# Two edits of order in a two-block transformer kernel: the opening (small loads behind the first roundings, more identity turns), and the place of the last maxima of each attention head on VectorE

## The reference

```python
def rmsnorm(x, g):
    xf = x.astype(jnp.float32)
    y = xf * lax.rsqrt(jnp.mean(xf * xf, axis=-1, keepdims=True) + EPS)
    return (y * g.astype(jnp.float32)).astype(x.dtype)

def even_mixer(h, layer, w_in, ...):
    p = jnp.einsum('bsd,de->bse', h, w_in)
    da_q, da_k, da_v, da_z, ml_qk, ml_v, ml_i, ml_f, ml_o, ml_z = _split(p, EVEN_SIZES)
    lam = (exp(dot(lambda_q1, lambda_k1)) - exp(dot(lambda_q2, lambda_k2)) + lam_init)
    ...
        s = jnp.einsum('bhcqd,bhckd->bhcqk', qi, kt)          # qi scaled, 8 heads, c = 2
        s = jnp.where(k_pos[None, :] <= q_pos[:, None], s, -jnp.inf)
        p = jax.nn.softmax(s, axis=-1)
        a = p[:, :, 0] - lam * p[:, :, 1]
        return jnp.einsum('bhqk,bhkv->bhqv', a, vt)
    ...
    o_a = rmsnorm(o_a, da_head_g) * (1.0 - lam_init)
    y_a = o_a.reshape(B, S, DA_WIDTH) * jax.nn.silu(da_z)
```

## Time and profile before

| | us |
|---|---|
| median of 3 runs | 2017.31 |
| lowest, highest | 2015.11, 2018.63 |
| the profiled execution | 2014.95 |
| its span | 2013.2 |
| PE busy | 1969.5 (98%) |
| DVE busy | 1058.4 (53%) |
| ACT busy | 737.1 (37%) |
| POOL busy | 66.7 (3%) |
| mean granted clock of PE | 0.991 |

### The profile page before, as it was taken

How to read it: one execution, slowest core, us unless ns; L and a number is a source line. 1 busy time by engine, 2 the same in 40 slices (tenths; PEclk the granted TensorE clock), 3 DMA queues, 4 the chain that set the end, 5 groups by cost and what they waited for, 6 DMA issues and landing times.

```text
span 2013.2 us, 30871 instructions
## 1 busy us (share of the span) xinstructions
PE 1969.5 (98%) x11878; PEld 1692.0 (84%) x11878; DVE 1058.4 (53%) x1618; ACT 737.1 (37%) x1158; POOL 66.7 (3%) x112
## 2 busy tenths in 40 slices
PE   7999998999999999999999999999999999999998
PEld 6777776888887888888899999999999889999886
DVE  4666666666525355553354555555576364444433
ACT  4433333332223333232335455555553243233222
POOL 2000000000002000000110000000000020000000
PEclk8999998999999999999999999999999999999999
DMA  5222211222232333223232222222222323333321
GB/s 162 74 63 73 63 53 53 74 73 63 87 112 73 110 91 92 86 91 115 63 112 78 74 74 74 74 74 67 71 74 74 105 74 94 94 94 94 101 98 52
DMA packets 244001, 167.24 MB, mean 83 GB/s; under 512 B 5293, under 2 KB 231701, under 8 KB 243910
## 3 DMA queue, kind: packets, MB, share of 16 engines
q1 hardware_dynamic: 242224, 160.98, 27.0%
q10 hardware_dynamic: 1286, 4.23, 0.7%
q0 software_dynamic: 400, 0.72, 0.1%
HBM read 163.81 MB, written 2.10 MB: 82 GB/s over the span
## 4 chain that ended last, share of the span: by engine, by line
PE 79%; issue 18%; DVE 2%; ACT 1%; DMA 0%; POOL 0%; ACTq 0%; SPq 0%; POOLq 0%; DVEq 0%
PE pj L1658 9%; PE pj L1660 9%; PE pj L1659 9%; PE pj L1211 5%; PE pj L1212 5%; PE pj L1210 5%; PE zz L1211 2%; PE zz L1210 2%; PE zz L1212 2%; PE pj L1267 2%; PE pj L1268 2%; PE pj L1269 2%; PE zz L1267 2%; PE zz L1269 2%; PE zz L1268 2%
## 5 line engine op out<-in xcount | busy, mean ns | idle before, releaser
L1978 DVE TENSOR_TENSOR w_lo<-raw,w_hi 128x1024 fp32r<-128x1024 f32 x299 | 365.1, 1222 | 300.3 <-ACT w_hi L634 296.7
L634 ACT ACTIVATE w_hi<-raw 128x1024 fp32r<-128x1024 f32 x299 | 314.6, 1053 | 211.5 <-PE tr L1269 139.1
L1658 PE MATMUL pj<-x_hi,w_hi 128*128 128x258 f32 (+1 forms) x1280 | 367.2, 287 | 0.0
L1659 PE MATMUL pj<-x_lo,w_hi 128*128 128x258 f32 (+1 forms) x1280 | 361.5, 282 | 0.0
L1660 PE MATMUL pj<-x_hi,w_lo 128*128 128x258 f32 (+1 forms) x1280 | 361.5, 282 | 0.0
L1210 PE MATMUL pj<-x_hi,w_hi 128*128 128x512 f32 x760 | 308.5, 406 | 1.7 <-ACT gate L703 1.7
L1211 PE MATMUL pj<-x_lo,w_hi 128*128 128x512 f32 x760 | 303.0, 399 | 0.0
L1212 PE MATMUL pj<-x_hi,w_lo 128*128 128x512 f32 x760 | 300.7, 396 | 0.0
L1659 PEld LDWEIGHTS pj<-x_lo,w_hi 128*128 128x128 f32 x1280 | 241.9, 189 | 0.8
L1658 PEld LDWEIGHTS pj<-x_hi,w_hi 128*128 128x128 f32 x1280 | 241.5, 189 | 1.1
L1660 PEld LDWEIGHTS pj<-x_hi,w_lo 128*128 128x128 f32 x1280 | 241.9, 189 | 0.0
(11 more groups left out here) (576 smaller groups left out, 3501.4 us busy)
## 6 DMA issues: line engine op xcount, KB each, us to landing
raw<-in_l_w_in_dram SPq DMA_DIRECT2D x113, 512.0 KB, 4.0
raw<-in_w_in_dram SPq DMA_DIRECT2D x64, 512.0 KB, 4.0
raw<-in_w_up_gate_dram SPq DMA_DIRECT2D x44, 512.0 KB, 3.8
raw<-in_l_w_out_dram SPq DMA_DIRECT2D x32, 512.0 KB, 3.4
raw<-in_w_down_dram SPq DMA_DIRECT2D x22, 512.0 KB, 3.3
raw<-in_w_proj_conv_dram SPq DMA_DIRECT2D x8, 512.0 KB, 3.8
raw<-in_w_proj_attn_dram SPq DMA_DIRECT2D x8, 512.0 KB, 3.7
raw<-in_w_out_dram SPq DMA_DIRECT2D x8, 512.0 KB, 3.3
```

Of the source, the lines that this page charges most:

```text
L634: act.activation(w_hi[:, slot], raw[:, slot], ACT.Copy).then_inc(hi_done, 1)
L1658: pe.matmul(dst, w_hi[:, slot, k, :], hi[:, k, tok], start=(k == 0), stop=False)
L1659: pe.matmul(dst, w_hi[:, slot, k, :], lo[:, k, tok], start=False, stop=False)
L1978: dve.tensor_tensor(w_lo[:, slot], raw[:, slot], w_hi[:, slot].bitcast(F32), ALU.subtract).then_inc(lo_done, 1)
```

## The change

In the opening: 36 identity turns instead of 20, and 8 and 26 more behind the turns of rows 0 and 1; PE multiplies the gate tile with the first half of the tokens before it turns rows 2 and 3. ACT's small loads go behind the roundings, and its splits of the first two weight tiles go between those; DVE's splits likewise, with the scaling of row 2 behind them. ACT copies the gate rows before it takes the exp of lambda. DVE splits the fourth tile before the small columns.

In the attention, on DVE alone: the maxima of block 3 go from block 0 of the next head to block 3 of this one, ahead of `y_lo` and `vtok`; `zs` goes from block 3 to block 0 of the next head, behind the `combine` there.

```diff
@@ -26,7 +26,8 @@
 MASKED = -1e30
 LAM_INIT = 0.8 - 0.6 * math.exp(-0.3 * 0)
 NSLOT = 4
-WARM = 20
+WARM = 36
+WARM_ROWS = (8, 26, 0, 0)
 AHEAD = 3
 
 
@@ -677,32 +678,30 @@
             act.activation(ms[:], half[:], ACT.Square)
             for t in range(NT):
                 square_row(0, t)
+            round_row(0, 0)
+            split(G_0)
+            round_row(0, 1)
+            split(G_0 + 1)
+            for j, v in enumerate((l0_lambda_q1, l0_lambda_k1, l0_lambda_q2, l0_lambda_k2)):
+                act.dma_start(lamv[:, j, :], v.rearrange("(a d) -> a d", a=1)).then_inc(S["first_in"], 16)
+            round_row(0, 2)
+            round_row(0, 3)
             for name, src in ROWS[0]:
                 a = col[name][1]
                 act.dma_start(vrow[a:a + src.shape[0], 0, :], src).then_inc(S["first_in"], 16)
-            round_row(0, 0)
-            for j, v in enumerate((l0_lambda_q1, l0_lambda_k1, l0_lambda_q2, l0_lambda_k2)):
-                act.dma_start(lamv[:, j, :], v.rearrange("(a d) -> a d", a=1)).then_inc(S["first_in"], 16)
-            round_row(0, 1)
-            split(G_0)
-            split(G_0 + 1)
-            round_row(0, 2)
             for j, v in enumerate((l0_b_igate, l0_b_fgate)):
                 act.dma_start(bif[:, j:j + 1], v.rearrange("(d a) -> d a", a=1)).then_inc(S["first_in"], 16)
-            round_row(0, 3)
             split(G_0 + 2)
             act.wait_ge(S["meta_in"], 32)
             act.activation(squares0[0:NM, :], mt[:], ACT.Square, scale=D ** -0.5,
                            accum_out=m_ms[:, 0:1]).then_inc(S["meta_step"], 1)
-
-            act.wait_ge(S["lam_step"], LAM_STEP["products"])
-            act.activation(lame[:], aux[:, 0, 8:10], ACT.Exp).then_inc(S["lam_step"], 1)
-
             split(G_0 + AHEAD)
             finished(G_0)
             act.activation(gate[:], pj[0:2 * HM, 0, :], ACT.Copy).then_inc(G["copied"], 1)
             act.wait_ge(G["copied"], 1)
             act.dma_start(gf[:], gate[HM:2 * HM, :]).then_inc(G["moved_f"], 16)
+            act.wait_ge(S["lam_step"], LAM_STEP["products"])
+            act.activation(lame[:], aux[:, 0, 8:10], ACT.Exp).then_inc(S["lam_step"], 1)
             act.wait_ge(S["meta_step"], SETUP_META["turned"])
             act.activation(x_hi[:, :, 0:NM], rb[:, 0, 0:KD * NM].rearrange("p (k t) -> p k t", k=KD),
                            ACT.Copy).then_inc(S["meta_step"], 1)
@@ -1302,19 +1301,28 @@
             pe.wait_ge(S["consts"], 1)
             for k in range(WARM):
                 pe.transpose(pj[:, 0, 0:P], ident[:], ident[:])
-            for t in range(NT):
-                if t == NT - 1:
-                    pe.wait_ge(*x_ready(0, 0))
+            def keep_turning(n):
+
+                for k in range(n):
+                    pe.transpose(pj[:, 0, 0:P], ident[:], ident[:])
+
+            halves0 = [slice(NM, NM + T // 2), slice(NM + T // 2, TF)]
+
+            def first_part(b, hf):
+                part(G_0 + b, pj[:, b, hf * (T // 2):(hf + 1) * (T // 2)], x_hi, x_lo, halves0[hf],
+                     tile_done if hf else None, start=(hf == 0))
+
+            for t in range(2):
                 turn_row(0, t)
-
+                keep_turning(WARM_ROWS[t])
             pe.wait_ge(*x_ready(0, 1))
-            halves0 = [slice(NM, NM + T // 2), slice(NM + T // 2, TF)]
-            for hf in range(2):
-                if hf:
-                    pe.wait_ge(*x_ready(0, NT - 1))
-                for b in range(2):
-                    part(G_0 + b, pj[:, b, hf * (T // 2):(hf + 1) * (T // 2)], x_hi, x_lo, halves0[hf],
-                         tile_done if hf else None, start=(hf == 0))
+            first_part(0, 0)
+            turn_row(0, 2)
+            turn_row(0, 3)
+            first_part(1, 0)
+            pe.wait_ge(*x_ready(0, NT - 1))
+            first_part(0, 1)
+            first_part(1, 1)
 
             pe.wait_ge(S["first_in"], 16 * N_FIRST_LOADS)
             pe.wait_ge(S["rows_in"], 16 * N_ROW_LOADS)
@@ -2024,10 +2032,10 @@
             scale_row(0, 0)
             scale_row(0, 1)
             rest_row(0, 0)
+            split(G_0)
+            rest_row(0, 1)
+            split(G_0 + 1)
             scale_row(0, 2)
-            rest_row(0, 1)
-            split(G_0)
-            split(G_0 + 1)
             scale_row(0, 3)
             rest_row(0, 2)
             rest_row(0, 3)
@@ -2036,6 +2044,7 @@
             dve.wait_ge(S["meta_step"], SETUP_META["power"])
             dve.scalar_tensor_tensor(xmeta[:], mt[:], m_ms[:, 1:2], gmeta[:], ALU.mult,
                                      ALU.mult).then_inc(S["meta_step"], 1)
+            split(G_0 + AHEAD)
             dve.wait_ge(S["turned"], 1)
             for r, n in enumerate(nrows):
                 ins = dve.tensor_copy(cols[r][:], tt[:, 0, r * P:r * P + n])
@@ -2055,7 +2064,6 @@
             dve.wait_ge(S["lam_step"], LAM_STEP["exp"])
             dve.scalar_tensor_tensor(lam[:], lame[:, 0:1], LAM_INIT, lame[:, 1:2], ALU.add,
                                      ALU.subtract).then_inc(S["lam_step"], 1)
-            split(G_0 + AHEAD)
             dve.wait_ge(S["meta_step"], SETUP_META["rounded"])
             raw_meta = rb[:, 0, KD * NM:2 * KD * NM].rearrange("p (k t) -> p k t", k=KD)
             dve.tensor_copy(hmf[:], raw_meta[:, :, A0:NM])
@@ -2129,13 +2137,16 @@
                 dve.tensor_copy(paT[:, 0:qt + 1, :].rearrange("p a b -> p (a b)"),
                                 tt[:, 0, 0:(qt + 1) * P]).then_inc(DA["probsT"], 1)
 
+            def gate_z(hd, par):
+                dve.wait_ge(DA["tanh"], hd + 1)
+                dve.scalar_tensor_tensor(zs[:, par, :], tz[:], 1.0, pj[:, (D_0 + 3) % 2, :], ALU.add,
+                                         ALU.mult).then_inc(DA["zs"], 1)
+
             def head(hd, par, proj=True, prev=True, prev2=True):
                 for b in range(4):
                     if b == 3 and prev2:
                         dve.wait_ge(DA["power"], hd - 1)
                         diagonals(odg_hi, odg_lo, DA["diag"])
-                    if b == 0 and prev2:
-                        maxima(hd - 2, NT - 1)
                     if b > 0 and prev:
                         maxima(hd - 1, b - 1)
                     if b < 2 and prev2:
@@ -2146,6 +2157,8 @@
                         combine(hd - 2, NT - 1)
                     if b > 0 and prev:
                         combine(hd - 1, b - 1)
+                    if b == 0 and prev:
+                        gate_z(hd - 1, 1 - par)
                     if proj:
                         split(D_0 + b + AHEAD, hd, 4)
                     elif b % 2:
@@ -2163,6 +2176,9 @@
                         dve.wait_ge(DA["spread"], hd - 1)
                         link(dve.scalar_tensor_tensor(ysb[:], o_sb[:], gda[:], rb[:, 0, :], ALU.mult, ALU.mult))
                         dve.tensor_tensor(ysb[:], ysb[:], zs[:, par, :], ALU.mult).then_inc(DA["y"], 1)
+                    if b == 3 and prev:
+                        maxima(hd - 1, NT - 1)
+                    if b == 3 and prev2:
                         dve.wait_ge(DA["yhi"], hd - 1)
                         dve.tensor_tensor(y_lo[:, bass.ds(hd - 2, 1), :], ysb[:].unsqueeze(1),
                                           y_hi[:, bass.ds(hd - 2, 1), :].bitcast(F32),
@@ -2172,9 +2188,6 @@
                         if prev2:
                             dve.wait_ge(DA["pv"], (hd - 1) * NT)
                         dve.tensor_copy(vtok[:, par].rearrange("p a b -> p (a b)"), aux[:, 0, :]).then_inc(DA["vtok"], 1)
-                        dve.wait_ge(DA["tanh"], hd + 1)
-                        dve.scalar_tensor_tensor(zs[:, par, :], tz[:], 1.0, pj[:, (D_0 + 3) % 2, :], ALU.add,
-                                                 ALU.mult).then_inc(DA["zs"], 1)
 
             dve.wait_ge(S["lam_step"], LAM_STEP["lam"])
             head(0, 0, prev=False, prev2=False)
```

## The result

| | before | after |
|---|---|---|
| median, us | 2017.88 (2015.11 to 2018.63, 4 runs) | 2004.26 (2002.84 to 2005.67, 4 runs) |
| ratio, 95% interval | | 0.9934 (0.992 to 0.9949) |
| profiled execution, its span | 2014.95, 2013.2 | 2002.84, 2001.1 |
| mean granted clock of PE | 0.991 | 0.994 |

The change made the kernel faster by 13.6 us by the medians and 12.1 us by the two profiled executions. The forecast was 12.7 us less, and 2004.6 us.

The account below looks back on a forecast made before the run. The prediction took TensorE (PE), busy 98% of the span, as the bound. Opening 7.4 plus attention 5.3 made 12.7 us, taken from the median 2017.31 to forecast 2004.6 us, range 2000 to 2012.5.

Parts of the forecast that it names:

- (a): Opening: 36 identity turns end at 10.1 to 10.4, or 11.65 at slow pace; cost 0 to 0.4 us, hidden.
- rival A: Opening: identity turns don't hold the clock; the opening loses 0.5 us, time 2012.5 us; chance 0.10.
- (b): Opening: first weight tile lands at 13.8, roundings and splits follow, PE's products start at 17.3 instead of 22.20.
- (c): Opening: PE stays occupied with 256-column products and two row turns, ending at 30.8 instead of 34.95; 4.15 us gained.
- (d): Opening: the gate copy, now ahead of lambda's exp, runs during the small turns; its wait of 1.69 us goes.
- (e): End of the opening: without the gate-copy standstill the clock doesn't fall a second time, saving 1.5 us.
- The small loads: Opening: issued behind row 3's rounding, about 23 to 26; cost taken as 0, 1.8 us if they land late.
- rival C: Opening: small loads come late, PE waits from 30.8 until 32.5 and the clock falls; time 2007.9 us; chance 0.10.
- The seven heads: Attention: earlier maxima make pa ready with 2 us to spare, so PE's waits for it go; 4.4 us.
- rivals B: Attention: the wait moves because something else paces the heads; only the opening pays, 2009.9 us; chance 0.12.
- D: Attention: zs becomes the bound, PE waits 2.4 us or more in each of 7 heads; 2026.9 us; chance 0.04.
- Head 1 and head 2: Attention: a new 1.2 us wait at the gate columns, while waits of 1.0 and 1.1 go; 0.9 us gained.

Follow-up runs that it names:

- e3: The changed kernel with 20 identity turns at the start and none between the rows, one execution: 2006.52 us.
- e12: The changed kernel with 20 identity turns at the start and none between the rows, as in e3, five executions: median 2004.32 us.
- e6: The changed kernel with zs back at the end of block 3, only the maxima moved, one execution: 2001.31 us.
- e4: The changed kernel with the five vector loads back ahead of row 0's rounding on ScalarE's queue, one execution: 2001.21 us.
- e10: The changed kernel unchanged, measured again over five executions: median 2002.76 us, ratio 0.993.

## Why the prediction was right

**(a), the identity turns, and rival A.** Right. The 36 end at 10.7, a little behind the estimate (they ran slow for longer), and it costs nothing, as the bound of 11.65 allowed. They hold the clock at 1.00 from 10 us on; without them it is 0.50 up to 22 us in e3, and in e12 the pace is slow up to 20 us.

**(b) and (c), the products.** Right: the weight tile landed at 13.55 (13.8 in the reckoning), the products started at 17.12 (17.3). The part (c) gave 4.56 us (34.95 to 30.39) instead of 4.15; the two row turns took 1.66 and not 2.0, since both ran at the full clock.

**(d), the gate copy.** Right: ScalarE copies at 27.66, PE doesn't wait, 1.7 us. (c) and (d) together are the 6.32 us of the ledger's first row, 5.85 forecast.

**(e), the second fall of the clock.** This is the step that failed. I reckoned that without a standstill the clock would not fall, and put 1.5 us on it. It fell near 34 us in four of the five traces of this opening, without a standstill ahead of it. From the first 512-column product to the 60th it is 15.25 us before, 15.34 after the change and 13.81 in e6: in the profiled execution the term was worth nothing, in e6 its full size. So the size, 1.5, was right and the condition was wrong: a standstill is not needed. Before the change the fall came at about 38.6 us (the clock reads 0.65 in 38 to 40), at the end of the wait for the gate copy, which made the wait look like its cause; but the small turns stood ahead of it there too. The opening gave 6.2 us in the profiled execution and 8.0 (54.04 to 46.04) in e6; the forecast of 7.4 lies between them by luck.

**The small loads, rival C.** Right that they cost nothing: they are issued from 22.02 to 24.3, and the turns that need them don't wait at 30.39. e4 adds that their old place had cost nothing either: I had put the late rounding of row 0 down to them, and the weight tile's landing hid it.

**The seven heads, rivals B and D.** Right in mechanism, `pa` 2.1 us early (2 forecast), `zs` far from being a bound. The size was 4.4 and is 4.98 (11.84 - 6.86). The reason is how idle time is counted: a stop's idle time begins at the modelled end of the matmul before it, but without the stop the next matmul begins ahead of that end. Before, from the start of the last scores to the turn it was 1.22 us (158.08 to 159.30) and now it is 0.42 (150.54 to 150.96): 0.80 for a wait shown as 0.73. Seven times 0.07 to 0.08 is the missing 0.5 us.

**Head 1 and head 2.** The new wait at the gate columns was forecast at 1.2 and is 1.35, and `pa` came 0.17 too late for head 2's turns where I had them level. Net 0.63 instead of 0.9.

**The sum.** 6.2 + 0.6 + 5.0 + 0.3 behind it = 12.1 us against 12.7. The mis-sized terms nearly cancel: the clock is down by 1.6 and head 1 by 0.3; the rest of the opening is up by 0.5, the seven heads by 0.6, and 0.3 behind them had no term. That the median came within 0.4 us of 2004.6 is therefore partly luck, and so is the basis: the median before moved from 2017.31 to 2017.88 with a fourth execution.

## What to carry to other kernels

Read from the profile which input ends the wait before the first product, and take out of its way everything else; what is merely late, like the small loads here, is worth nothing. On VectorE, order the links of a chain that PE waits for ahead of copies whose reader comes later, and look for the once-only work (here the gate rows between head 1 and the loop) that the same move pushes into a wait. A stretch of idle PE is worth its idle time and a little more, because the pipelined start is lost too; and if PE must wait early in a kernel, turns of the identity can keep its clock up. Here they brought the first large product 1.5 to 2.5 us forward, and in four of six executions a later fall of the clock took 1.5 us back.

## What was not expected of the hardware

The granted clock fell without an idle stretch before it, and not in every execution of the same code: it did in those where the pace had risen late at the start. Each such fall costs about 1.5 us (34 to 36 at 0.50, its neighbours at 0.89 and 0.75). Others come later: in stretches of 100 us the profiled execution of e10 shows 0.98 in 1400 to 1500, 1500 to 1600 and 1600 to 1700, that of the change in the first of these three alone, and they end with spans of 2003.9 and 2001.1 although up to 302 us they differ by 0.4. Two falls more, at about 1.5 us each, account for the 2.8 us between these two. That falls of the clock also make the spread of 3 to 5 us among the other executions is likely, but only the profiled ones have a trace. One execution therefore can't price a part of 1 us by its total time; the distance between two instructions on PE on either side of the part can, and it was the same to 0.01 us (40.34 twice).
